# Recurrence in chunks: v centred before the recurrence, one read of two PSUM banks for a pair of heads, and a later logarithm

## The reference, cut to what matters

```python
def step(state, inp):
    r_t, w_t, k_t, v_t, aa_t, bb_t = inp
    sa = jnp.einsum('bhij,bhj->bhi', state, aa_t)
    state = (state * w_t[:, :, None, :] + sa[..., None] * bb_t[:, :, None, :]
             + v_t[..., None] * k_t[:, :, None, :])
    y = jnp.einsum('bhij,bhj->bhi', state, r_t)
    return state, y
...
mu = jnp.mean(y, axis=-1, keepdims=True)
var = jnp.mean(jnp.square(y - mu), axis=-1, keepdims=True)
yn = (y - mu) * lax.rsqrt(var + GN_EPS)
yn = yn * gn_w + gn_b
bonus = jnp.sum(r_h * k_h * r_k.astype(jnp.float32), axis=-1, keepdims=True) * v_h
out = (yn + bonus) * heads(g)
```

## Time and profile before

| | |
|---|---|
| median of three executions | 3264.36 us |
| the profiled execution, its own time | 3259.7 us |
| its span, first to last instruction | 3257.9 us |
| mean granted clock of TensorE | 0.984 |
| recurrence, units 0 to 7, on TensorE | 2020.22 to 2355.73 us, 335.5 us |
| TensorE busy over the span | 3078.1 us (94%) |
| VectorE, ScalarE busy over the span | 1979.6 us (61%), 1417.1 us (43%) |

### The profile page before, as it was taken

How to read it: one execution, slowest core, us unless ns; L and a number is a source line. 1 busy time by engine, 2 the same in 40 slices (tenths; PEclk the granted TensorE clock), 3 DMA queues, 4 the chain that set the end, 5 groups by cost and what they waited for, 6 DMA issues and landing times.

```text
span 3257.9 us, 46321 instructions
## 1 busy us (share of the span) xinstructions
PE 3078.1 (94%) x18478; PEld 2345.0 (72%) x18478; DVE 1979.6 (61%) x3370; ACT 1417.1 (43%) x2611; POOL 0.2 (0%) x4
## 2 busy tenths in 40 slices
PE   8988999999999999899999999888899999999888
PEld 7446666688888887778888666666646887787766
DVE  3635667667666656875555476666543666656675
ACT  2313555645333334553334455555412554444343
POOL 0000000000000000000000000000000000000000
PEclk9999999999999999999999899999999999999999
DMA  7510000042333356543333400000043334455545
GB/s 272 194 46 1 1 1 1 13 155 68 94 104 97 104 173 220 178 153 98 118 109 107 164 17 18 22 20 17 19 157 137 126 106 144 142 184 203 185 164 181
DMA packets 254519, 351.27 MB, mean 108 GB/s; under 512 B 12384, under 2 KB 142048, under 8 KB 251104
## 3 DMA queue, kind: packets, MB, share of 16 engines
q1 hardware_dynamic: 254304, 348.30, 32.0%
HBM read 263.84 MB, written 84.41 MB: 107 GB/s over the span
## 4 chain that ended last, share of the span: by engine, by line
PE 73%; DVE 11%; DMA 8%; issue 4%; ACT 3%; SPq 0%; DVEq 0%; ACTq 0%
PE ps L198 71%; DMA wr<-in_w_down 6%; DVE wl L406 3%; DMA hid<-ob 2%; PE ps L1572 1%; DVE NM L2429 1%; PE ps L934 1%; ACT wh L382 1%; PE ps L2868 0%; DMA wr<-hid 0%; DVE MM L3187 0%; DVE ob L1325 0%; DVE Yf L507 0%; DVE QT L2448 0%; DVE RT L2447 0%
## 5 line engine op out<-in xcount | busy, mean ns | idle before, releaser
L198 PE MATMUL ps<-ffn_h,wh 128*128 128x512 f32 x2176 | 672.9, 390 | 12.4 <-DVE ob L1325 9.2
L406 DVE TENSOR_TENSOR wl<-wr,wh 128x512 fp32r<-128x512 f32 x610 | 403.2, 688 | 276.0 <-ACT wh L382 272.5
L382 ACT ACTIVATE wh<-wr 128x512 fp32r<-128x512 f32 x610 | 363.9, 624 | 459.7 <-PE ps L198 280.4
L198 PEld LDWEIGHTS ps<-ffn_h,wh 128*128 128x128 f32 x2176 | 408.0, 188 | 101.7 <-DVE ob L1325 13.5
L198 PE MATMUL ps<-ffn_h,wl 128*128 128x512 f32 x1088 | 423.9, 390 | 0.0
L198 PE MATMUL ps<-in_h,wh 128*128 128x512 f32 x1200 | 371.0, 390 | 4.5 <-DVE Yf L836 4.5
L198 PE MATMUL ps<-wh,wh 128*128 128x512 f32 x756 | 301.5, 399 | 46.1 <-DVE wl L406 46.0
L198 PE MATMUL ps<-wl,wh 128*128 128x512 f32 x756 | 298.3, 395 | 0.0
L198 PE MATMUL ps<-wh,wl 128*128 128x512 f32 x756 | 298.1, 394 | 0.0
L198 PEld LDWEIGHTS ps<-in_h,wh 128*128 128x128 f32 x1200 | 225.8, 188 | 52.2 <-DVE Yf L836 4.9
L198 PEld LDWEIGHTS ps<-ffn_h,wl 128*128 128x128 f32 x1088 | 204.6, 188 | 42.9
(11 more groups left out here) (370 smaller groups left out, 5126.1 us busy)
## 6 DMA issues: line engine op xcount, KB each, us to landing
hid<-ob SPq DMA_DIRECT2D x174, 256.0 KB, 2.3
wr<-hid SPq DMA_DIRECT2D x84, 512.0 KB, 4.4
wr<-in_w_down SPq DMA_DIRECT2D x72, 512.0 KB, 3.7
wr<-in_w_up SPq DMA_DIRECT2D x54, 512.0 KB, 4.3
wr<-in_w_in SPq DMA_DIRECT2D x42, 512.0 KB, 5.1
kept<-ob SPq DMA_DIRECT2D x84, 256.0 KB, 2.0
late<-in_w_ada SPq DMA_DIRECT2D x16, 1024.0 KB, 7.2
wr<-in_w_out SPq DMA_DIRECT2D x32, 512.0 KB, 4.2
```

Of the source, the lines that this page charges most:

```text
L198: return e.op.matmul(out, left, right, start=start, stop=stop, skip_group_check=True)
L382: e.op.activation(self.rows(s)[0], src, ACT.Copy).then_inc(*e.event(self.name + "_act", ("w_high", self.name, s)))
L406: e.op.tensor_tensor(lo, src, hi.bitcast(F32), ALU.subtract).then_inc(*e.event(self.name + "_dve", ("w_low", self.name, s), *done))
```

## The change

There are three edits, all in the recurrence.

1. `v_rows` is made by four matmuls against a constant matrix `centre` (identity minus 1/64 within each head) where it was four transposes, so the copied block holds centred `v`. The product `mean` and the subtraction L3332 are gone; `yc` is written by the addition after `yt`, and the square follows it.
2. Steps move between rounds. On ScalarE the logarithm and exponential of the group norm go from round 14 to 16 (counted from 0), the square from 12 to 11, the scaling from 16 to 18, and `ahead` now stands ahead of `behind` in a round. `b_rows` goes from round 19 to 16 on TensorE, and to 17 on ScalarE; `k_rows` from 20 to 18 and 19. On VectorE `k_end` goes from round 19 to 16, and the three last steps of the group norm from 15, 17, 18 to 17, 19, 20. The output gate's product goes from round 16 to 17.
3. The matrices of the two heads lie in one tile (`[128, 2, 4, 64]`), and one instruction reads both banks of a set in place of one per bank: 256 and 256 columns become 512, 512 and 512 become 1024. It waits for both heads' products, and the next set's products wait for it.

```diff
+    put("centre", (r == q) - (r // 64 == q // 64) / 64.0)
...
@@ enter_tensor
-        self.rows_tensor(e, j, "v_rows", lambda i: v[:, i * 128:(i + 1) * 128], ("shifted", "v", j))
+        group = ("v_rows", j)
+        _, free = k.settle(group, 6)
+        e.wait_ge(free, ("shifted", "v", j))
+        for i in range(4):
+            x = mm(e, k.out(group, 128, 128 * i), v[:, i * 128:(i + 1) * 128], k.cst("centre"), True, True)
+        x.then_inc(*e.event("mix_mm", ("mm", group)))
...
         self.rows_tensor(e, j, "a_rows", ...)
-        for _ in range(4):
-            yield
+        yield
         self.rows_tensor(e, j, "b_rows", lambda i: a_[:, i * 128:(i + 1) * 128], ("b_end", j))
         yield
+        yield
         self.rows_tensor(e, j, "k_rows", lambda i: k_[:, i * 128:(i + 1) * 128], ("k_end", j))
...
+    def both(self, group, a=0, b=64, n=64, at=0):
+
+        o = self.k.bank_of[group] * 512
+        return self.k.ps[:, o:o + 1024].rearrange("p (s x) -> p s x", s=2)[:, :, at:at + 4 * n].rearrange("p s (u n) -> p s u n", u=4)[:, :, :, a:b]
...
@@ chunk_scalar
         def keep(what, dst, a=0, b=64, n=64, after=None):
-            for s in range(2):
-                e.wait_ge(("mm", name(s, what)), (after, name(s, what)) if after else None)
-                e.op.activation(dst(s), self.four(name(s, what), a, b, n), ACT.Copy).then_inc(*e.event("chunk_act", ("read", name(s, what))))
+            e.wait_ge(*both("mm", what), *(both(after, what) if after else []))
+            e.op.activation(dst, self.both(("chunk", j, 0, what), a, b, n), ACT.Copy).then_inc(*e.event("chunk_act", *both("read", what)))
...
@@ chunk_vector
         def added(what, dst, n, event="read", wide=None):
-            for s in range(2):
-                e.wait_ge(("mm", name(s, what)))
-                o = dst[s][:, :, 0:n]
-                e.op.tensor_tensor(o, self.four(name(s, what), 0, n, wide or n), o, ALU.add).then_inc(*e.event("chunk_dve", (event, name(s, what))))
+            e.wait_ge(*both("mm", what))
+            o = dst[:, :, :, 0:n]
+            e.op.tensor_tensor(o, self.both(("chunk", j, 0, what), 0, n, wide or n), o, ALU.add).then_inc(*e.event("chunk_dve", *both(event, what)))
...
@@ leave_tensor
-        self.sums_tensor(e, ("mean", j), 7, Yt[:, :], ("read", ("yt", j)))
...
@@ leave_scalar
-        for _ in range(12):
+        for _ in range(11):
             yield
-        e.wait_ge(("read", ("mean", j)), ("mm", ("mean", j)))
+        e.wait_ge(("read", ("yt", j)))
         e.op.activation(Yt[:, :], yc[:, :], ACT.Square).then_inc(*e.event("mix_act", ("centred_sq", j)))
-        yield
-        yield
+        for _ in range(5):
+            yield
         e.wait_ge(("mm", ("var", j)))
...
@@ leave_vector
-        e.op.tensor_tensor(Yt[:, :], k.out(("yt", j)), self.Y0[:, sl], ALU.add).then_inc(*e.event("mix_dve", ("read", ("yt", j))))
-        yield
-        e.wait_ge(("mm", ("mean", j)), ("read", ("yt", j)))
-        e.op.scalar_tensor_tensor(yc[:, :], k.out(("mean", j)), -1.0 / 64, Yt[:, :], ALU.mult, ALU.add).then_inc(*e.event("mix_dve", ("read", ("mean", j))))
+        e.op.tensor_tensor(yc[:, :], k.out(("yt", j)), self.Y0[:, sl], ALU.add).then_inc(*e.event("mix_dve", ("read", ("yt", j))))
...
@@ scalar
-            together(*behind, *ahead, self.chunk_scalar(e, j))
+            together(*ahead, *behind, self.chunk_scalar(e, j))
```

More of the change, by code:

```diff
@@ L2925, in enter_scalar @@
         yield
+        self.rows_copy(e, j, "b_rows", self.Btm)
         yield
         yield
-        self.rows_copy(e, j, "b_rows", self.Btm)
+        self.rows_copy(e, j, "k_rows", self.Ktm)
         yield
-        self.rows_copy(e, j, "k_rows", self.Ktm)
         yield
@@ L3044, in prod @@
                 done(x, s, what)
-        A, Aoff, A2, N4, GT, G, NR, KR, XN, WU = zip(*self.mats)
+        A, Aoff, A2, N4, GT, G, NR, KR, XN, WU = [[t[:, s, :, :] for s in range(2)] for t in self.mats]
         X, N2 = [t[:, :, 0:64] for t in XN], [t[:, :, 64:128] for t in XN]
@@ L3160, in chunk_scalar @@
         yield
[L3161 to L3164, removed]
+        e.wait_ge(*both("mm", "out"), *both("r2", "out"), *self.left(j - 2))
+        e.op.activation(self.by_parity(self.Y0, j), self.both(("chunk", j, 0, "out"), at=256), ACT.Copy).then_inc(*e.event("chunk_act", *both("read", "out")))
         yield
[L3166 to L3169, removed]
+        e.wait_ge(*both("mm", "state"), *both("mt", "state"), *self.left(j - 2))
+        e.op.activation(self.by_parity(self.NN, j), self.both(("chunk", j, 0, "state"), at=256), ACT.Copy).then_inc(*e.event("chunk_act", *both("read", "state")))
         yield
@@ L3189, in chunk_vector, with masked @@
-        for s in range(2):
-            masked("a", s, A, "mA16", 64, "a16")
+        A, Aoff, A2, N4, GT, G, NR, KR, XN, WU = self.mats
+        both = lambda way, what: [(way, ("chunk", j, s, what)) for s in range(2)]
+        bc = lambda c, n: k.cst(c).unsqueeze(1).unsqueeze(1).broadcast_to([128, 2, 4, n])
+        def masked(what, dst, m, n, event):
+            e.wait_ge(*both("mm", what))
+            e.op.tensor_tensor(dst[:, :, :, :], self.both(("chunk", j, 0, what), 0, n, n), bc(m, n), ALU.mult).then_inc(
+                *e.event("chunk_dve", *both(event, what)))
@@ L3191, in chunk_vector @@
+        def added(what, dst, n, event="read", wide=None):
+            e.wait_ge(*both("mm", what))
+            o = dst[:, :, :, 0:n]
+            e.op.tensor_tensor(o, self.both(("chunk", j, 0, what), 0, n, wide or n), o, ALU.add).then_inc(*e.event("chunk_dve", *both(event, what)))
+        masked("a", A, "mA16", 64, "a16")
         yield
-        for s in range(2):
-            masked("nr", s, NR, "mNR", 128, "read")
+        masked("nr", NR, "mNR", 128, "read")
         yield
-        for s in range(2):
-            masked("a", s, Aoff, "mAoff", 64, "read")
+        masked("a", Aoff, "mAoff", 64, "read")
@@ L3197, in chunk_vector @@
         yield
-        for s in range(2):
-            e.wait_ge(("read", name(s, "nr")))
-            e.op.tensor_tensor(XN[s][:, :, 0:64], NR[s][:, :, 0:64], bc("id64", 64), ALU.add).then_inc(*e.event("chunk_dve", ("x1", name(s, "nr"))))
+        e.wait_ge(*both("read", "nr"))
+        e.op.tensor_tensor(XN[:, :, :, 0:64], NR[:, :, :, 0:64], bc("id64", 64), ALU.add).then_inc(*e.event("chunk_dve", *both("x1", "nr")))
         yield
-        for s in range(2):
-            masked("kr", s, KR, "mKR", 128, "read")
-            yield
@@ L3205, in chunk_vector @@
-        e.wait_ge(*[("x1", name(s, "nr")) for s in range(2)])
+        masked("kr", KR, "mKR", 128, "read")
+        yield
+        yield
+        e.wait_ge(*both("x1", "nr"))
         added("xn4", XN, 64, "x2", 128)
         yield
-        e.wait_ge(*[("x2", name(s, "xn4")) for s in range(2)])
+        e.wait_ge(*both("x2", "xn4"))
         added("x4", XN, 64)
@@ L3212, in chunk_vector @@
         yield
-        e.wait_ge(*[("read", name(s, "x4")) for s in range(2)])
+        e.wait_ge(*both("read", "x4"))
         added("x8", XN, 64)
@@ L3336, in leave_vector @@
         yield
-        e.wait_ge(("group_rstd", j), ("read", ("mean", j)))
+        yield
+        yield
+        yield
+        e.wait_ge(("group_rstd", j), ("read", ("yt", j)))
         e.op.tensor_tensor(yc[:, :], yc[:, :], Yt[:, :], ALU.mult).then_inc(*e.event("mix_dve", ("normed", j)))
```

81 lines of the change are left out of this document (33 added, 48 removed).

## The result

The changed kernel is slower: median 3361.12 us (3351.68 to 3381.88, 4 executions) against 3267.85 (3263.5 to 3279.54, 4) of the kernel before, run beside it; ratio 1.0288, 95% interval 1.0229 to 1.0348. The forecast was 3249, with a range from 3238 to 3262; the measured time lies far above both. The profiled execution took 3367.7 us, its span 3365.9, 108.0 longer than before.

What follows compares the result with a forecast made beforehand. TensorE, 94% busy, was taken as the bound through its waits for copies and additions. 6 x -3.0 + 3.1 + 0 - 1.05 + 0.3 = -15.7 us from 3259.7 gives 3244.0, as a median 3249; range 3238 to 3262.

Steps and rivals of the forecast that it cites:

- The first `v_rows` beside the attention: Unit 0's `v_rows` as float32 matmuls during the attention: costs 0 to 0.45 us, taken as 0.3.
- The walk: Step-by-step timing of middle unit 4 from its decay product: 41.7 us after the change against 44.7.
- x4: TensorE product set in a unit's first half: waits for one addition covering both heads, +0.75 us for what follows.
- wait before b_rows: New TensorE wait of 1.4 us after `g2`, until ScalarE has copied `a_rows` out of bank 6.
- rate: Product at the next unit's head: needs bank 7 from the output gate's multiplication, starts at 42.25, wait about 1 us.
- 6 x -3.0: Term for units 1 to 6 of the recurrence: each 3.0 us shorter, 44.7 to 41.7.
- first rival: Clock still falls around `a_rows` and `b_rows` in the middle units: 1.7 us a unit stay lost, 3259; chance 0.12.
- The second rival: At the unit's end VectorE's queue slips 1 to 1.5 us, delaying `rate`; units gain 1.5 to 2, 3256; chance 0.12.
- The third rival: Lost overlap of heads also shows at n2, a4, a8, akv, x8: 4.4 us a unit, total 3275; chance 0.08.
- Unit 0: First unit of the recurrence, without a group norm to fill gaps: loses 3.1 us.
- Unit 7: Last unit: losses at x4, y1, y2 and last copies balance gains in `mean`, `var` and y1's wait: 0.
- The gates: Unit 7's group norm beside the gates, where TensorE never stops: removing `mean` gains its full 1.05 us.

Runs made afterwards that it cites:

- experiment 1: The changed kernel with unit 0's `b_rows`, `k_rows` and `k_end` back in their old rounds; 3266.88 us, ratio 1.0019 to the kernel before.
- experiment 5: The changed kernel without merged reads (centred `v` and new order only), unit 0's rows in their old rounds; 3241.46 us, ratio 0.9896 to the kernel before.
- experiment 3: The kernel before with the merged reads of both heads alone, all rounds as before; 3296.82 us, ratio 1.0119.
- experiment 7: The kernel before with the new order of steps alone, unit 0's rows in their old rounds; 3251.0 us, ratio 0.9945.
- experiment 2: The kernel before with only unit 0's `b_rows`, `k_rows` and `k_end` in their new rounds; 3366.65 us, ratio 1.0331.

## Why the prediction was wrong

**The step that failed.** "The first `v_rows` beside the attention costs 0 to 0.45, taken as 0.3." That was all the prediction had for unit 0's preparation, and it weighed only what is added there. `b_rows` was moved past three attention items as well, and its wait for ScalarE, which I had worked out for the middle units (1.4), was not looked for there. It was 1.87 us, and its price was not 1.87 but about 94 of the 110.3 by which the recurrence begins later: the clock behind it. None of the four rivals had this place. Without it, experiment 1 lands at 1.0019: 3264.36 x 1.0019 = 3270.6, still above the range. So a second, smaller error stands behind the first: the recurrence gained 3.4 us, not 15.

**The middle units.** The walk, against unit 3 (us from the unit's start):

| | forecast | measured |
|---|---|---|
| x4 | 12.04 | 13.36 |
| x8 | 17.95 | 19.50 |
| gt | 19.9 | 21.54 |
| a_rows | 25.8 | 27.52 |
| wait before b_rows | 1.4 | 1.25 |
| y1, y2 | 29.35, 32.8 | 31.08, 34.56 |
| out | 36.25 | 37.94 |
| rate | 42.25 | 43.58 |

Every wait was there, at nearly its size but for that of `rate`, 0.35 for about 1. `a` already starts 0.8 later in the unit since `rate` begins late at its head, so 0.8 of each difference in the table stands there before the walk begins; x4 adds 0.5. The unit is 42.11 for 41.7. The term "6 x -3.0" of the sum was mis-sized for two reasons. First the scaling: 3.0 us is unit 4's gain from 44.70, but the six units before had 264.8 in all, 44.1 each. Six units of 41.7 would gain 14.6, not 18; measured are 253.3 (2172.26 to 2425.58), a gain of 11.4. Second, the walk ended the unit 0.55 ahead of `rate`, as if decay and rate ran one after the other. Before, their four matmuls take 1.13 together; in the changed kernel the four take 1.94 at 2255.95, and the two of decay alone 1.12 at 2298.06. So a late `rate` costs nearly its whole delay. A unit ended at `rate`, 42.25, lies next to the measured mean of 42.2; that it fits so well is in part luck, since x4 came later and `rate` waited less than the walk had it.

**The clock, first rival.** In five of six units it doesn't fall, as forecast. In unit 4 it does, behind three stretches in which TensorE stands still: 0.83 before out, 0.95 in which the profile shows nothing that it waited for, and 0.35 before `rate`:

```profile
2299.50:2306.50 7.00, 6.97 (x114) 5.40 (x116) 3.24 (x6) 2.72 (x4) 0.00 (x0) 0.52 0.01 2
```

This unit takes 44.15, some 2 us more than its neighbours; experiment 1 has the same there (44.16, clock 0.92). Why this unit and not the others is open. By the transposes' rule of the Trainium skill quoted in the prediction ("TensorE: Matmul & The Clock Gate", Part 4: PE-mode transpose) the row `a_rows`, g2, wait, `b_rows` would have made a fall likelier in every unit. The traces don't bear that out for this row: the clock is 1.00 in unit 3 with all of them in it, and where it falls, in unit 4, it falls at the unit's start, 13 us behind unit 3's `b_rows` and long ahead of unit 4's.

**The second rival** (`rate` slips by a further 1 to 1.5 us) didn't show: the wait was 0.35 us, less than the walk's own. That the units gained 1.9 each, as it had it, comes from the two sizes above.

**The third rival, the other side,** was nearest in direction. Merging costs 27.0 / 8 = 3.4 us a unit, 2.7 in the unit compared. But it costs at the places that the walk had charged, not at ScalarE's copies n2, a4, a8: merging ScalarE's reads costs 3.1 us in all eight units, which is within what equal code differs by. The rule of the Trainium skill ("Perfetto Trace Analysis", Optimizing Scalar/DVE Operations) that I set against the merging is borne out for VectorE's reads: 304.0 us with all reads broken up, 326.2 with VectorE's merged, 331.0 with all merged. I had it and gave it 0.08, since I walked the three edits as one. Priced apart, the merging was a loss by my own charges (+0.75 at x4, +0.3 at x8, the uncovered additions at gt and y2) with nothing on the other side but cheaper instructions on engines that have time.

**Unit 0** lost 5.5, not 3.1; in experiment 1, where no attention at half clock precedes it, it takes 40.21, a loss of 4.0. **Unit 7** lost 2.5, not 0: the wait at its start for ScalarE's merged copy of unit 6's `state` (L3164) was missed; the one at its end, 1.02 before, was charged.

```profile
2427.52 1.10 PE L199 MATMUL ps<-AR,F 64*64 64x128 f32 x32 [1.30 <-ACT F L3164]
...
2462.61 5.40 PE L199 MATMUL ps<-yaT,PW 128*128 128x512 f32 x8 [1.51 <-ACT F L3164]
```

**The gates.** The piece of the chain that answers to the earlier trace rows is 112.92 us with 312 matmuls against 113.75 with 314: 0.83 less for a forecast of 1.05. It is lost again just ahead of it, where the last row above takes 5.40 us for eight matmuls that took 3.70 before: the granted clock is 0.50 from 2463.6 to 2466.6. What brings it down is open: experiment 5 has 5.40 behind a wait of 1.03, experiment 3 has 3.70 behind one of 1.52.

**Durations.** 1024 columns take 1.23 us on VectorE, as estimated:

```profile
L3181 DVE TENSOR_TENSOR MM<-ps,MM 128x1024 f32<-128x1024 f32 x12 | 14.7, 1225 | 36.8 <-PE ps L199 36.8
```

The sum of the span: +110.3 to the recurrence's start (94 by the wait, 16 with the longer first fall), -3.4 in it (units 1 to 6 -11.4, unit 0 +5.5, unit 7 +2.5), +1.1 behind it: +108.0.

**Not settled.** Why the attention, once at half clock, comes back after 20 us in one execution, after 45 in another and not at all in a third. In the trace of experiment 7 it fell again at about 1922 with no wait longer than 0.34 us on TensorE in the 10 us before. So the wait of 1.87 us is enough for the fall (all 8 executions with it have the long time, where kernels without it have it in 33 of 136, and the two traces show the fall at its end), but not needed for it.

## What to carry to other kernels

When a step moves, walk it in every stage in which it runs, the first and last iterations too: a preparation that overlaps another stage meets that stage's queues there. Price edits apart and look for one that only pays inside a sum: merging two reads saves instructions on engines that have time to spare, and takes away the start of the next half on the engine that has none. Here merging VectorE's masks and additions cost 22.2 us, and merging ScalarE's copies neither a clear cost nor a gain.

## What was not expected of the hardware

A single idle stretch of 1.87 us on TensorE was followed by 185 us at 1.2 GHz in which it was busy for every microsecond; at that clock it is the bound of the attention, with VectorE busy for 66 us of 185 and ScalarE for 56. In the recurrence, idle stretches of 3.16 us cost no more than the few us of the earlier trace rows before the clock was back, and in the trace of experiment 2 the one that ends at 2266.72 was followed by 10 us at 1.00. So what an idle stretch cost depended on what ran behind it: about 94 us of clock in the attention, 1.7 us or nothing in the recurrence.
